# The conv stage of a hybrid diffusion step in seven block products instead of eight

## The reference

```python
proj = h @ lw['w_in']                       # h: 640 x 1024
bg, cg, u_in, cq_raw, ckv_raw, kr, g_conv, g_mla = jnp.split(proj, idx, axis=-1)
u = jnp.pad(cg * u_in, ((0, 0), (1, 1), (0, 0)))
w = lw['conv_w']
conv = u[:, :-2] * w[0] + u[:, 1:-1] * w[1] + u[:, 2:] * w[2]
y_conv = (bg * conv) @ lw['w_conv_out']
...
y_mla = attend(q_nope, q_rope, k_nope, kr_all, v_h) @ lw['w_o']
merged = jax.nn.sigmoid(g_conv) * y_conv + jax.nn.sigmoid(g_mla) * y_mla
return merged @ lw['w_mix_out'], ckv, kr
```

## Time and profile before

| | us |
|---|---|
| median of 3 runs | 918.02 (917.73 to 918.52) |
| span of the profiled execution | 916.3 |
| TensorE busy | 874.4 |
| VectorE busy | 421.8 |
| ScalarE busy | 276.0 |
| GpSimd busy | 110.5 |

### The profile page before, as it was taken

One profiled execution on the slowest core, in us unless ns is written; L12 is line 12 of the kernel. 1 busy time (PEld: TensorE's weight loads), 2 busy tenths in 40 slices (PEclk: granted clock), 3 DMA queues, 4 the chain that ended last, 5 costly groups with the idle time before them and its releaser, 6 DMA issues. The chain is left out here.

```text
span 916.3 us, 15131 instructions
## 1 busy us (share of the span) xinstructions
PE 874.4 (95%) x6078; PEld 694.8 (76%) x6078; DVE 421.8 (46%) x907; ACT 276.0 (30%) x522; POOL 110.5 (12%) x123
## 2 busy tenths in 40 slices
PE   5999999999999999999999999993999999999996
PEld 4787777888899999999999998882555555555551
DVE  3667355555444252433513195368443443434333
ACT  5357654655411212112122132333111111111123
POOL 0000000000000000000000040201223333332320
PEclk9999999999999999999999999996899999999999
DMA  9972624602313222122141148669899999999948
GB/s 333 352 289 99 242 107 161 209 23 69 107 47 92 60 77 92 46 92 92 46 161 46 47 152 249 186 266 354 348 415 415 416 414 415 413 414 417 414 163 343
DMA packets 73681, 198.86 MB, mean 217 GB/s; under 512 B 11384, under 2 KB 43112, under 8 KB 61080
## 3 DMA queue, kind: packets, MB, share of 16 engines
q1 hardware_dynamic: 65800, 181.71, 53.8%
q0 software_dynamic: 7824, 16.36, 4.8%
HBM read 189.30 MB, written 18.17 MB: 226 GB/s over the span
## 5 line engine op out<-in xcount | busy, mean ns | idle before, releaser
L819 PE MATMUL pair<-w_ug,xgT 128*64 128x256 f32 x1184 | 138.1, 386 | 1.3 <-ACT xgT L956 1.3
L1748 ACT CAST hi<-raw 128x2048 fp32r<-128x2048 f32 (+3 forms) x31 | 53.8, 1735 | 224.8 <-PE pair L1356 202.1
L1352 PE MATMUL pair<-hT,hi 128*128 128x320 f32 x512 | 116.8, 309 | 0.0
L1356 PE MATMUL pair<-hT,lo 128*128 128x320 f32 x512 | 116.7, 309 | 0.0
L1354 PE MATMUL pair<-hT,hi 128*128 128x320 f32 x512 | 116.6, 309 | 0.0
L819 PEld LDWEIGHTS pair<-w_ug,xgT 128*64 128x64 f32 x1184 | 84.7, 139 | 42.0 <-issue 4.4
L1930 DVE TENSOR_TENSOR lo<-raw,hi 128x2048 fp32r<-128x2048 f32 (+2 forms) x30 | 65.6, 2188 | 109.2 <-ACT hi L1748 108.4
L1352 PEld LDWEIGHTS pair<-hT,hi 128*128 128x128 f32 x512 | 85.7, 188 | 0.2 <-issue 0.2
L1354 PEld LDWEIGHTS pair<-hT,hi 128*128 128x128 f32 x512 | 85.6, 188 | 0.0
L1356 PEld LDWEIGHTS pair<-hT,lo 128*128 128x128 f32 x512 | 85.5, 188 | 0.0
L838 PE MATMUL pair<-w_dn,actT 128*64 128x512 f32 x296 | 71.7, 605 | 1.3 <-issue 0.9
(11 more groups left out here) (355 smaller groups left out, 1474.2 us busy)
## 6 DMA issues: line engine op xcount, KB each, us to landing
w_ug<-in_w_up SPq DMA_DIRECT2D x32, 1024.0 KB
w_ug<-in_w_gate SPq DMA_DIRECT2D x32, 1024.0 KB
w_dn<-in_w_down SPq DMA_DIRECT2D x32, 1024.0 KB
raw<-in_w_in SPq DMA_DIRECT2D x20, 1024.0 KB, 5.3
ada_a<-in_w_ada SPq DMA_DIRECT2D x14, 1024.0 KB, 12.1
raw<-in_w_ada SPq DMA_DIRECT2D x10, 1024.0 KB, 5.7
ya<-expert_rows SPq DMA_DIRECT2D x5, 1024.0 KB, 9.0
raw<-in_w_conv_out SPq DMA_DIRECT2D x4, 1024.0 KB, 5.0
```

Source lines behind the costliest of these rows:

```text
L819: x = pe.matmul(bank[2 + d % 2][g * SL:(g + 1) * SL, 0:DE], xgT[d % 2][:, k, h * SL:(h + 1) * SL], w_ug[r][:, g, h, k, :], start=(n == 0), ...
L1352: pe.matmul(o, st[0], m[0], start=first, stop=False)
L1356: x = pe.matmul(o, st[1], m[0], start=False, stop=last)
L1748: act.copy(hi[n % 2][:, 0:size], raw[n % 4][:, 0:size]).then_inc(hi_done, 1)
```

## The change

Each pass now has four products (`CG`, `UU`, `BG`, `GC`), and each product takes 128 columns `it*128` from the lower and 128 from the upper 512 columns of its 1024. The product of the 640 x 1024 activations with these 1024 x 256 weights is seen as one of 2 x 2 blocks: the tokens in halves of 320, the features in halves of 512, the columns in halves of 128. It is computed by seven block products ("units", 12 matmuls each) instead of eight, with three sums of blocks of the weights that GpSimd adds up in place (`w_sum`, four operations of 128 x 512), and four blocks of sums of the activations (`row_sum`, ten operations in two halves each, of 128 x 640) that GpSimd makes during the attention and the other engines split there. VectorE and ScalarE add the seven results up to the four blocks. The weights are loaded once, in quarters. The rest of the attention and what follows the conv stage are as before, apart from names, the place of the tiles in memory and semaphores that are shared by several uses. The first unit stands before the last transpose and the last value product of the attention. The diff, cut to its core:

```diff
+    unit_turn = {31 + g: g for g in range(4)}
+    sum_turn = {35: 0, 36: 1, 37: 2}
+    Q_B11, Q_B21, Q_SUM, Q_B22 = (slice(512 * q, 512 * (q + 1)) for q in range(4))
+    UNIT_SRC = (Q_B11, Q_SUM, Q_B21, Q_B22, Q_SUM, Q_B22, Q_SUM)
+    UNIT_SUM = (None, 0, None, None, 1, 2, 3)
...
+    A11, A12, A21, A22 = quarter(0, 0), quarter(0, 1), quarter(1, 0), quarter(1, 1)
+    UNIT_ROWS = (A11, (d_hi[0], d_lo[0]), A12, A21, (d_hi[1], d_lo[1]), (d_hi[2], d_lo[2]), A22)
...
+        for i in range(NPROD):
+            it, x, _, _ = product_of(i)
+            if i < 3:
+                sp.wait_ge(lo_done, N_GM + i + 1)
+            else:
+                sp.wait_ge(s_ulo, 7 * (i - 2))
+            dst = raw[i % 3]
+            sp.dma_start(v3(dst, KD, P), kpc(w_in[:, col_of(x) + it * P:col_of(x) + (it + 1) * P])
+                         ).then_inc(raw_in[i % 3], 16)
+            sp.dma_start(dst[:, Q_SUM].rearrange("p (k c) -> p k c", k=4), w_quarter(i, 0, 1)).then_inc(raw_in[i % 3], 16)
+            sp.dma_start(dst[:, Q_B22].rearrange("p (k c) -> p k c", k=4), w_quarter(i, 1, 1)).then_inc(raw_in[i % 3], 16)
...
+        SUMS = ((d0, a21[0], a22[0], 1), (d0, d0, a21[1], 0), (d0, d0, a22[1], 1),
+                (d1, a11[0], d0, 1), (d1, d1, a11[1], 0),
+                (d2, a21[0], a11[0], 1), (d2, d2, a21[1], 0), (d2, d2, a11[1], 1),
+                (d3, a12[0], d1, 1), (d3, d3, a12[1], 0))
+        def row_sum(n):
+            dst, x, y, less = SUMS[n]
+            for h in range(2):
+                ks = slice(2 * h, 2 * h + 2)
+                if n:
+                    pool.wait_ge(pchain, 2 * n - 1 + h)
+                op = pool.tensor_sub if less else pool.tensor_add
+                op(dst[:, ks, :], x[:, ks, :], y[:, ks, :]).then_inc(pchain, 1)
+        def w_sum(kind, i):
+            if kind == 0:
+                pool.wait_ge(raw_in[i % 3], conv_in_count(i))
+            else:
+                pool.wait_ge(s_ulo, 7 * i + (None, 2, 4, 5)[kind])
+            if kind == 2:
+                pool.wait_ge(*sum_done(1, i))
+            if kind == 3:
+                pool.wait_ge(*sum_done(2, i))
+            total, first, other = (raw[i % 3][:, q] for q in (Q_SUM, Q_B11, (Q_B11, Q_B22, Q_B22, Q_B21)[kind]))
+            if kind == 2:
+                x = pool.tensor_sub(other, total, first)
+            else:
+                x = pool.tensor_add(total, total, other)
+            x.then_inc(sum_done(kind, i)[0], 1)
...
+            if g == 8:
+                pool.wait_ge(s_sc, 4 * NT)
+            for n in range(max(4 * (g - 8), 0), min(4 * (g - 7), len(SUMS))):
+                row_sum(n)
+            if g == 10:
+                w_sum(0, 0)
+            if g == 14:
+                w_sum(0, 1)
+                w_sum(1, 0)
+            if g == 15:
+                w_sum(2, 0)
+        w_sum(3, 0)
+        for i in range(1, NPROD):
+            if i + 1 < NPROD:
+                w_sum(0, i + 1)
+            for kind in range(1, 4):
+                w_sum(kind, i)
...
+        def conv_product(g):
+            i, m = divmod(g, 7)
+            pe.wait_ge(s_ulo, g + 1)
+            if i == 0 and m in (1, 3, 4, 5):
+                pe.wait_ge(s_dlo, {1: 1, 3: 4, 4: 2, 5: 3}[m])
+            if m == 0:
+                if i == 0:
+                    pe.wait_ge(s_ex, len(units) - 1)
+                elif i == 1:
+                    pe.wait_ge(s_pe, len(units))
+                else:
+                    pe.wait_ge(s_comb, combined(i - 2, FIRST_N))
+            if m == 1:
+                if i == 1:
+                    pe.wait_ge(s_ol, NH)
+                elif i > 1:
+                    pe.wait_ge(s_comb, combined(i - 2, SECOND_N))
+            if m == 2:
+                pe.wait_ge(s_pcopy, 2 * i + 1)
+            if m == 3:
+                pe.wait_ge(s_pcopy, 2 * i + 2)
+            if m == 4:
+                if i == 0:
+                    pe.wait_ge(s_ex, len(units))
+                elif i == 1:
+                    pe.wait_ge(gm_copied, N_CHUNK)
+                else:
+                    pe.wait_ge(s_comb, combined(i - 2, BLK21))
+            if m == 5 and i >= 1:
+                it, x, _, _ = product_of(i - 1)
+                if x in (CG, GC):
+                    pe.wait_ge(s_act11, 3 * it + (1 if x == CG else 2))
+                else:
+                    pe.wait_ge(s_dve11, 2 * it + (1 if x == UU else 2))
+            if m == 6:
+                if i == 0:
+                    pe.wait_ge(s_pe, len(units))
+                else:
+                    pe.wait_ge(s_comb, combined(i - 1, BLK12))
+            w, rows, out = unit_w(g), UNIT_ROWS[m], prod_bank(i, UNIT_BANK[m])
+            for k in range(4):
+                x = prod(out, [t[:, k * P:(k + 1) * P] for t in w], [t[:, k, :] for t in rows],
+                         k == 0 and m not in (2, 3), k == 3, adds=m in (2, 3))
+            x.then_inc(s_pu, 1)
+        def last_units():
+            n = len(units) - 1
+            conv_product(0)
             p_turn(n)
-        pv(NH - 1)
-        with pe.Fori(0, 4) as it:
-            q = 0
-            for p in range(4):
-                n = N_CONV + p
-                pe.wait_ge(lo_done, it * 4 + (n + 1))
-                wv = [v3(t, KD, 256) for t in (hi[n % 2], lo[n % 2])]
-                for mm in range(2):
-                    pe.wait_ge(blk_free, it * 6 + max(q - 3, 0) + 1)
-                    if q == 2:
-                        pe.wait_ge(gc_free, it * 2 + 1)
-                        pe.wait_ge(s_ol, NH)
-                        pe.wait_ge(gm_copied, N_CHUNK)
-                    for k in range(KD):
-                        x = prod2(halves(q % 4), [t[:, k, mm * P:(mm + 1) * P] for t in wv],
-                                  [[hT(t, k)[:, c * HALF:(c + 1) * HALF] for t in range(2)] for c in range(2)],
-                                  k == 0, k == KD - 1)
-                    x.then_inc(piece_used if mm else blk_done, 1)
-                    q += 1
-        def gate_block(n, mm, kk, rhs, out):
+            pv(NH - 1)
...
+        def unit_hi(g):
+            i, m = divmod(g, 7)
+            if m == 0:
+                act.wait_ge(raw_in[i % 3], conv_in_count(i))
+            elif UNIT_SUM[m] is not None:
+                act.wait_ge(*sum_done(UNIT_SUM[m], i))
+            if g >= 8:
+                act.wait_ge(s_pu, g - 7)
+            else:
+                act.wait_ge(piece_used, N_GM + 3 + g // 4)
+            act.copy(unit_w(g)[0], unit_src(g)).then_inc(s_uhi, 1)
+        def sum_hi(d):
+            act.wait_ge(pchain, 20)
+            if d < 3:
+                act.wait_ge(s_sc, NT * (5 + d))
+                act.copy(d_hi[d][:, :, :], d_sum[d][:, :, :]).then_inc(s_dhi, 1)
+            else:
+                act.wait_ge(piece_used, N_G)
+                act.copy(A21[0], d_sum[3][:, :, :]).then_inc(s_dhi, 1)
...
+        conv_tail = {UNITS - 5: (0, 1), UNITS - 4: (2,), UNITS - 3: (3,), UNITS - 2: (4, 5), UNITS - 1: (6, 7)}
+        for g in range(UNITS):
+            i, m = divmod(g, 7)
+            it, x, j, j4 = product_of(i)
+            if m == 1:
+                act.wait_ge(s_pu, 7 * i + 1)
+                if i >= 2:
+                    act.wait_ge(s_comb, combined(i - 2, BLKS))
+                act.copy(p1_s[i % 2][:, :], prod_bank(i, 0)).then_inc(s_pcopy, 1)
+            if m == 2:
+                act.wait_ge(s_pu, 7 * i + 2)
+                act.copy(v_s[i % 2][:, :], prod_bank(i, 1)).then_inc(s_pcopy, 1)
+            if g + UAHEAD < UNITS:
+                unit_hi(g + UAHEAD)
+            if m == 3 and x == CG and i:
+                gate_conv(i - 1)
+            if m == 4 and x == CG:
+                act.wait_ge(s_pu, 7 * i + 3)
+                act.copy(conv[j][:, 0:HALF], prod_bank(i, 0)).then_inc(s_act11, 1)
+            for k in conv_tail.get(g, ()):
+                conv_hi(k)
+            if g == UNITS - 4:
+                split_hi(N_G, PIECE)
+        split_hi(N_G + 1, PIECE)
+        gate_conv(NPROD - 1)
...
+        def unit_lo(g):
+            w_hi, w_lo = unit_w(g)
+            dve.wait_ge(s_uhi, g + 1)
+            dve.tensor_sub(w_lo, unit_src(g), w_hi.bitcast(F32)).then_inc(s_ulo, 1)
...
+        def block11(i):
+            it, x, j, _ = product_of(i)
+            dve.wait_ge(s_pu, 7 * i + 3)
+            if x == UU:
+                dve.wait_ge(s_act11, 3 * it + 1)
+            times(x, j, prod_bank(i, 0), 0, U11).then_inc(s_dve11, 1)
+        def first_sum(i):
+            dve.wait_ge(s_pcopy, 2 * i + 1)
+            dve.wait_ge(s_pu, 7 * i + 5)
+            dve.tensor_sub(n_s[i % 2][:, :], prod_bank(i, 2), p1_s[i % 2][:, :]).then_inc(s_comb, 1)
+        def second_sum(i):
+            it, x, j, j4 = product_of(i)
+            p1, n2 = p1_s[i % 2][:, :], n_s[i % 2][:, :]
+            dve.wait_ge(s_comb, combined(i, FIRST_N))
+            dve.wait_ge(s_pu, 7 * i + 6)
+            dve.tensor_add(p1, prod_bank(i, 3), n2).then_inc(s_comb, 1)
```

(122 more changed lines are left out.)

337 lines of the change are left out of this document (188 added, 149 removed).

## The result

The changed kernel takes 925.35 us (median of 4 runs, 924.37 to 926.75) against 918.11 us (also a median of 4): **slower**, ratio 1.0075 with a 95% interval of 1.0060 to 1.0091. That is clear of the noise, though three quarters of a per cent only, and by a threshold of 2% it counts as "same". The prediction was 902.9 us and faster. The profiled span is 924.9 us, 8.6 us more than before.

What follows compares the result with a forecast made beforehand. TensorE's matmul count was taken to bound the conv stage. -28.15 + 6 + 2.5 + 2.5 + 1.5 + 0.5 = -15.15 us gave a span of 901.1 and a forecast of 902.9 us, range 888 to 916.

Steps and rivals of the forecast that it cites:

- So one of the two waits, whole instructions long, and they take turns: VectorE and GpSimd on shared SBUF access: they exclude each other, alternating by instruction; per pass 48.0 of 49.3 us.
- a VectorE instruction held up: Attention: GpSimd's row sums delay VectorE's scaled probabilities, which TensorE often takes at once; 2.5 us (0 to 7).
- the scaling, with one input in SBUF: Attention: no row showed it beside GpSimd; if held by the skill's rule, two costs grow some 4 us together, not summed.
- The store queue: Attention: gate chunk stores issued behind GpSimd's row sums hold up ScalarE's copies reusing the buffers; 2.5 us (0 to 7).
- splits of row sums: Attention, units 35 to 39: splitting four row sums adds work on ScalarE and VectorE; +1.5 us (0 to 4).
- the transition: End of attention: first unit fills TensorE's idle time, but the first `p_s` copy comes late; net +0.5 us (-1.2 to +3).
- Matmuls: Conv stage: 1344 matmuls instead of 1536 at 146.6 ns each, 28.15 us less; floor 197.1 us.
- start late: Rival, conv stage: each unit begins 0.1 us late on TensorE, 913.9 us; 16% together with heavier stalls.
- The wait behind `bg`: Conv stage: TensorE waits for ScalarE's copy before the next product's third unit; 1.5 us, four times, +6.
- The slower rival: Conv stage: every GpSimd sum holds VectorE, which becomes the bound; stage 224.8 us, total 927.6 us; 9%.

Runs made afterwards that it cites:

- e4: Changed kernel with each of GpSimd's twenty row-sum halves replaced by a copy of its first operand, queued the same way; 902.68 us, one run.
- e7: Changed kernel with a wait for the half directly before after every fourth row-sum half on GpSimd; 913.76 us, one run.
- e2: Changed kernel with each row-sum half on GpSimd waiting for the half directly before it, not the one before that; 899.44 us.
- e5: e3 with all 64 GpSimd weight sums left out; 904.72 us with tokens routed otherwise, so only its conv stage compares: 198.2 us against 203.15.
- e3: Changed kernel with row sums, and weight sums falling into the attention, spread over the attention's units; 895.74 us, 0.9751 of the kernel before.
- e6: e3 with the third tap and first block of `bg` moved behind their product's last split, second tap one unit later; 896.01 us.

## Why the prediction was wrong

- **The step that failed** is the sentence "So one of the two waits, whole instructions long, and they take turns". Whole instructions is right; the turns are no rule. At 533.74 us VectorE got in between two GpSimd subtractions, and I took this for one. The row sums of the changed kernel are of another kind: each waits for the half two before it, whose end comes as the one in front begins, and sixteen of them behind two stores let VectorE in nowhere. Why those two subtractions do let it in and these sums do not is open; the second subtraction waited for a cast of ScalarE that ended (534.63 us in the trace of before) only after the first had begun, and no store stood directly in front, and no run separates the two. From the rule I put "a VectorE instruction held up" at 2.5 us, with an upper end of 7, by the slack against a hold of 1.57 us; it was 23.2 us in one instruction, and 24.6 us of waits for TensorE. That row is one operation of 24.5 us to VectorE.
- That the scaling, with one input in SBUF, is held too was left open. It is: 23.23 us. The Trainium skill (SBUF — State Buffer, "SBUF: two separate sides") says that the pair of ports which GpSimd and some VectorE operations share is an exclusive lock, for the whole instruction, and counts operations in a two-port mode among those. The trace agrees that VectorE is fully blocked and that the scaling is among the blocked. The page speaks of one instruction; the changed kernel, e4 and three groups of e7 show VectorE kept out across the instructions of a row, and e2 that a wait between them lets it in.
- **The store queue** (2.5 us) did not exist: ScalarE waits for no store in the changed kernel, and once, 1.1 us, in e2. With the splits of row sums (1.5) and the transition (0.5) it makes 4.5 us; in e3 the attention with all of this takes 0.6 us less than before, and the transition's other end, the late first `p_s`, costs 1.3 us at the start of the conv stage. So these terms were priced too high.
- **Matmuls**: -28.15 us, right: the stage takes 198.2 us without weight sums (e5) against a floor of 197.1, 0.73 us of it the one wait, and the pitch is 146.6 ns. Units that wait for nothing do not start late.
- **The wait behind `bg`**: 1.5 us, four times, at the named instruction. Measured 1.09, 1.06 and 1.09 us behind the first three and 0.18 behind the last: 3.4 in place of 6. A wait of 1.33 us at the start, which the sum had under the transition, and about 1.3 us of slower restarts behind the five waits fill the gap; that the stage's total fits to 0.1 us is luck to this extent. e5 shows GpSimd's sums as its cause, as the working had it; e6 shows that relief at one place hands it on.
- **The slower rival** (VectorE as the bound of the conv stage, 927.6 us) gave nearly the measured time by a mechanism that did not occur: the stage took 203.15 and not 224.8 us.
- The clock was not in the sum. After the long wait TensorE worked at a granted clock of 0.50 for five microseconds (211 to 216 us); 24.6 us of waits became 29.5 us of loss.

## What to carry to other kernels

Elementwise work moved to GpSimd can cost VectorE a whole row of instructions that GpSimd runs without having to wait, not one instruction, above all, as far as these traces go, behind a store that GpSimd issues: put a wait for the instruction before, or better for an event of VectorE's own, ahead of each. Where two instructions in a trace take turns, look what each of them waited for and what stood in front before calling it a rule. An experiment that leaves out arithmetic ahead of a router changes the work behind it; compare its stages, not its total.

## What the hardware showed that was not expected

- VectorE's instruction beside a closed row of GpSimd operations: 23.2 us beside sixteen, 6.4 and 7.2 beside four and five; 1.6 to 1.9 beside single ones. A store issued by GpSimd between two of them (0.56 us) did not end the row.
- All fourteen rows that held VectorE to the end began directly behind a store issued by GpSimd. Rows without one let VectorE in between two operations although the second had nothing left to wait for (314.70 us in the changed kernel, its load landed at 308.39; the second and fourth group of e7). Whether the store is the cause was not tried.
- Copies by GpSimd with one input in SBUF shut out VectorE's scaling as well: 6.0 us beside eight of 0.67 us.
